# A decoder layer with 32 experts: w_down loaded once per expert, padding rows left out, the combine read with plain loads

## The reference

```python
h = rms_norm(x, g_pre_ffn[l]) * (1.0 + sc2) + sh2
y = hier_moe(h, ...)                    # below
x = x + gt2 * rms_norm(y, g_post_ffn[l])

# hier_moe: 4 groups of 8 experts, EXPERT_BLOCK = 128
group_p = softmax(ht @ w_rg + b_rg)              # top 1 group
e_prob, e_local = top_k(softmax(e_logit of that group), 2)
weights = g_prob * e_prob / sum(e_prob)
order = argsort(expert_ids)                      # 4096 assignments
padded = (counts + 127) // 128 * 128             # each expert: whole blocks of 128 rows
hb = silu(xb @ w_gate[e]) * (xb @ w_up[e])       # w_gate, w_up: 1024 x 256
y_block = hb @ w_down[e]                         # w_down: 256 x 1024
out = zeros.at[sorted_tok].add(y_sorted * weights)
```

## Time and profile before

| | us |
|---|---|
| median of 3 runs | 1963.77 |
| the profiled execution | 1967.04 |
| its span, first to last instruction | 1965.6 |
| PE busy | 1591.6 (81%) |
| DVE busy | 1313.0 (67%) |
| ACT busy | 844.5 (43%) |
| POOL busy | 260.1 (13%) |

### The profile page before, as it was taken

The page is one execution under the profiler, slowest core; times in us unless marked ns, Lnnn a source line. Parts: engine busy times, 40 slices in busy tenths (PEclk is TensorE's granted clock), DMA queues, the critical chain, the costliest instruction groups (busy, mean ns, idle before and its releaser), DMA issues. The chain is left out here.

```text
span 1965.6 us, 23849 instructions
## 1 busy us (share of the span) xinstructions
PE 1591.6 (81%) x7295; PEld 1179.9 (60%) x7296; DVE 1313.0 (67%) x1996; ACT 844.5 (43%) x1458; POOL 260.1 (13%) x382
## 2 busy tenths in 40 slices
PE   2698665799997999988999989377898888989800
PEld 2578544689565887657894644355676666766500
DVE  5399866599754699554996422675676666767556
ACT  1422330432545233534325323045666676767544
POOL 1000000000110000200001102121222222222164
PEclk7799856799987999978999889579999899999955
DMA  9254222231442332422311426459888878788677
GB/s 342 58 183 150 65 77 116 65 98 53 130 128 66 86 108 86 126 89 65 105 46 57 115 64 171 150 186 361 322 291 316 314 280 290 283 284 328 224 245 268
DMA packets 207655, 333.69 MB, mean 170 GB/s; under 512 B 7454, under 2 KB 155035, under 8 KB 207578
## 3 DMA queue, kind: packets, MB, share of 16 engines
q0 software_dynamic: 48704, 181.57, 27.3%
q1 hardware_dynamic: 158754, 151.09, 23.3%
q10 hardware_dynamic: 120, 0.04, 0.0%
HBM read 265.56 MB, written 67.11 MB: 169 GB/s over the span
## 5 line engine op out<-in xcount | busy, mean ns | idle before, releaser
L1634 DVE TENSOR_TENSOR w_rest<-wgu,w_high 128x1024 fp32r<-128x1024 f32 x192 | 232.1, 1221 | 168.2 <-ACT w_high L1560 167.3
L886 DVE SCALAR_TENSOR_TENSOR cv<-u,taps,cv 128x512 f32<-128x512 f32 x480 | 321.8, 747 | 0.6 <-DVE yT L842 0.3
L1560 ACT ACTIVATE w_high<-wgu 128x1024 fp32r x192 | 199.4, 1053 | 218.9 <-SPq L1424 156.2
L415 PE MATMUL bank<-hT_high,tiles_operand 128*128 128x512 f32 x512 | 204.5, 400 | 35.8 <-DVE hT_operand L860 21.1
L416 PE MATMUL bank<-hT_operand,tiles_operand 128*128 128x512 f32 x512 | 203.2, 397 | 0.0
L417 PE MATMUL bank<-hT_high,win_operand 128*128 128x512 f32 x512 | 202.4, 395 | 0.0
L438 PE MATMUL bank<-wo,yT 128*128 128x512 f32 x432 | 194.3, 606 | 0.0
L1520 PE MATMUL py<-wd,hTe 128*128 128x512 f32 x384 | 172.6, 592 | 0.6 <-DVE hTe L1657 0.6
L1509 PE MATMUL pgu<-w_high,x_high 128*128 128x512 f32 x384 | 161.1, 420 | 0.0
L1510 PE MATMUL pgu<-w_rest,x_high 128*128 128x512 f32 x384 | 155.5, 405 | 0.0
L1511 PE MATMUL pgu<-w_high,x_rest 128*128 128x512 f32 x384 | 153.6, 400 | 0.0
(11 more groups left out here) (326 smaller groups left out, 2785.6 us busy)
## 6 DMA issues: line engine op xcount, KB each, us to landing
wd<-w_down_in POOLq DMA_DIRECT2D x48, 1024.0 KB, 7.2
win<-w_in_in SPq DMA_DIRECT2D x64, 512.0 KB, 5.2
wgu<-w_gate_in SPq DMA_DIRECT2D x32, 1024.0 KB, 11.4
wgu<-w_up_in SPq DMA_DIRECT2D x32, 1024.0 KB, 13.6
y_dram<-yb POOLq DMA_DIRECT2D x48, 512.0 KB, 7.7
wo<-w_ada_in POOLq DMA_DIRECT2D x8, 2048.0 KB, 9.4
win<-w_in_in SPq DMA_DIRECT2D x16, 1024.0 KB, 5.3
y_dram<-zeros POOLq DMA_DIRECT2D x32, 512.0 KB, 7.7
```

What stands on the lines that cost most here:

```text
L415: nc.tensor.matmul(out[:], high[:, k, cols], hT_high[:, k, :], start=(k == 0), stop=False)
L886: ins = V.scalar_tensor_tensor(out=cv[:, j], in0=u[:, j, w:w + T], scalar=tap, in1=cv[:, j], op0=ALU.mult, op1=ALU.add)
L1560: A(w_high[:, QK * q:QK * q + QK, :], c.wgu[:, bass.ds(slot, 1), QK * q:QK * q + QK, :].rearrange("p a k n -> p (a k) n"), ACT.Copy).then_ ...
L1634: V.tensor_tensor(w_rest[:, part, :], c.wgu[:, bass.ds(slot, 1), part, :].rearrange("p a k n -> p (a k) n"), w_high[:, part, :].bitcast(F3 ...
```

## The change

- Experts are numbered by rank: the rank-th expert that has rows (the first three are always listed). Three tables, made in the routing, give the rank and slot of a block, the expert of a rank and the last block of a rank. The number of blocks is rounded up to even by giving the last expert one more.
- w_down has three slots, like gate/up, and is loaded by SP once per expert. SP's order per rank is in `serve`. PE reads the rank's table before every `down` (`rank_of`).
- Padding rows get a token number out of bounds, which the gather skips (`bounds_check`); `xg` is zeroed once. A block's result is scattered to y by assignment (k x 2048 + token) with an indirect store that skips padding. No zeros are stored any more.
- The combine reads the two halves of y with plain loads on SP, 8 buffers deep.
- In the mixer the bias is added by DVE when the logits are saved, so that the matmul of L456 goes, and `outputs` makes the full-width matmuls of all heads first, then those of the one half, then those of the other.
- The semaphores of the mixer are cleared at the routing.

```diff
@@ mixer, PE @@
                 for k in range(KD):
-                    nc.tensor.matmul(out[:, 0:NR], yt[:, i % 2, k * P:(k + 1) * P], c.wroute[:, k, :], start=(k == 0), stop=False)
-                nc.tensor.matmul(out[:, 0:NR], c.ones[0:1, :], c.brow[:], start=False, stop=True).then_inc(logit_ready, 1)
+                    last = nc.tensor.matmul(out[:, 0:NR], yt[:, i % 2, k * P:(k + 1) * P], c.wroute[:, k, :], start=(k == 0), stop=(k == KD - 1))
+                last.then_inc(logit_ready, 1)
...
+                cols_of = lambda h: slice(h * P, (h + 1) * P)
                 for h in range(NH):
-                    hc = slice(h * P, (h + 1) * P)
-                    nc.tensor.matmul(pO[:, hc], c.scoreT[:, i % 2, hc], v[:, i, hc], start=True, stop=False, skip_group_check=True)
-                    for s in range(2):
-                        at = i * P + s * CH
-                        last = nc.tensor.matmul(pO[s * CH:(s + 1) * CH, hc], qd[:, h, at:at + CH],
-                                                c.state[:, (2 * i + s) % 4, hc], start=False, stop=(s == 1), skip_group_check=True)
+                    nc.tensor.matmul(pO[:, cols_of(h)], c.scoreT[:, i % 2, cols_of(h)], v[:, i, cols_of(h)],
+                                     start=(h == 0), stop=False, skip_group_check=True)
+                for s in range(2):
+                    at = i * P + s * CH
+                    for h in range(NH):
+                        last = nc.tensor.matmul(pO[s * CH:(s + 1) * CH, cols_of(h)], qd[:, h, at:at + CH],
...
@@ routing @@
             for e in range(WSLOTS):
                 load_gate_up(sp, ap, c, e, e)
+                load_down(sp, ap, c, e, e)
...
-            L(V.tensor_tensor(cmp_[:], x32[2][:].unsqueeze(1).to_broadcast([P, TAB, NE]), bc(blk[:], NE), ALU.is_le))
-            L(V.tensor_reduce(etab[:], cmp_[:], axis=AX.X, op=ALU.add))
...
+            V.tensor_copy(c.rank_expert[:], pk[:, 0:NE])
+            V.tensor_copy(c.rank_end[:], pk[:, NE:2 * NE])
+            V.tensor_copy(c.block_rank[:], pk[:, 2 * NE:2 * NE + TAB])
...
+            L(V.tensor_scalar(c.block_assign[:], pi[:, 0:TAB], float(2 * SEQ), None, ALU.add))
+            L(V.tensor_scalar(c.block_token[:], c.block_assign[:], 2 * SEQ + SEQ - 1, None, ALU.bitwise_and))
...
@@ experts, SP @@
-            def announce(s, turn):
-                sp.wait_ge(c.w_in[s], 32 * turn)
-                sp.sem_inc(gate_up_loaded, 1)
-
-            def replace(e, s):
-
-                last = sp.value_load(c.block_end[0:1, bass.ds(e, 1)], min_val=1, max_val=4 * NBLK + 1)
-                wait_apart(sp, w_rest_ready, last, sp_passed)
-                load_gate_up(sp, ap, c, e + WSLOTS, s)
+            def announce(loaded, landed, n):
+                sp.wait_ge(landed, n)
+                sp.sem_inc(loaded, 1)
+
+            def next_gate_up(r, s):
+
+                e = expert_at(r + WSLOTS)
+                wait_apart(sp, w_rest_ready, 4 * end_of(r) + 1, sp_passed)
+                load_gate_up(sp, ap, c, e, s)
+
+            def next_down(r, s):
+
+                e = expert_at(r + WSLOTS)
+                wait_apart(sp, y_ready, 2 * end_of(r) + 1, sp_passed)
+                load_down(sp, ap, c, e, s)
...
+            def serve(r, s, turn):
+                early = isinstance(r, int) and r < WSLOTS
+                announce(gate_up_loaded, c.gu_in[s], 32 * turn)
+                if isinstance(r, int) and r == WSLOTS:
+                    for n in range(2):
+                        next_down(n, n)
+                announce(down_loaded, c.wd_in[s], 16 * turn)
+                if not isinstance(r, int) or r + WSLOTS < NE:
+                    next_gate_up(r, s)
+                if not early and (not isinstance(r, int) or r - 1 + WSLOTS < NE):
+                    next_down(r - 1, (s - 1) % WSLOTS)
...
+            with sp.Fori(2, ROUNDS) as g:
+                for s in range(WSLOTS):
+                    serve(g * WSLOTS + s, s, g + 1)
+                load_x1(g)
...
@@ experts, POOL @@
-            def load_down(b, s):
-                e, _ = expert_of(pool, b)
-                pool.dma_start(c.wd[:, s], ap["w_down"][0][bass.ds(e, 1)].rearrange("a (k p) n -> p (a k) n", p=P)).then_inc(wd_in[s], 16)
-
-            def store(b, s):
+            def store(b, s, n):
+                if not (isinstance(n, int) and n == 0):
+                    wait_apart(pool, y_stored[s], 16 * n, pool_passed)
+                nc.gpsimd.tensor_copy(places[:, s:s + 1], c.block_assign[:, bass.ds(b, 1)]).then_inc(place_copied, 1)
+                pool.wait_ge(place_copied, b + 1)
                 wait_apart(pool, y_saved, 2 * b + 3, pool_passed)
-                pool.dma_start(ap["y"][bass.ds(b * P, P), :], yb[:, s]).then_inc(y_stored[s], 16)
+                pool.indirect_dma_start(ap["y"], bass.IndirectOffsetOnAxis(places[:, s:s + 1], 0), yb[:, s], None,
+                                        bounds_check=2 * SEQ - 1, oob_is_err=False).then_inc(y_stored[s], 16)
...
@@ experts, PE @@
-            def down(b, s, times):
+            def down(b):
+                r, slot = rank_of(pe, b)
                 pe.wait_ge(hT_ready, b + 1)
-                pe.wait_ge(wd_in[s], 16 * times)
+                pe.wait_ge(down_loaded, r + 1)
                 pe.wait_ge(y_saved, 2 * b + 1)
...
@@ combine @@
-        RING = 4
+        RING = 8
...
+            def load(i, s):
+                for k, (buf, done) in enumerate(((ya, ya_in), (yb, yb_in))):
+                    sp.dma_start(buf[:, s], ap["y"][k * SEQ + i * P:k * SEQ + (i + 1) * P, :]).then_inc(done[s], 16)
+
+            for s in range(RING):
+                load(s, s)
+            for i in range(NTILES):
                 wait_apart(sp, out_ready, i + 1, sp_passed)
-                sp.dma_start(out[bass.ds(i * P, P), :], c.x1_all[:, bass.ds(i, 1)].rearrange("p a n -> p (a n)")).then_inc(out_stored, 16)
+                sp.dma_start(out[i * P:(i + 1) * P, :], c.x1_all[:, i]).then_inc(out_stored, 16)
+                if i + RING < NTILES:
+                    load(i + RING, i % RING)
```

More of the change, by code:

```diff
@@ L543, in last_modulation @@
                 last.then_inc(row_done, 1)
+                pe.wait_ge(bias_ready, 1)
+                nc.tensor.matmul(bank[3][:, 0:NR], c.ones[0:1, :], c.brow[0:1, :], start=True, stop=True).then_inc(row_done, 1)
                 pe.wait_ge(mod_ready, 2)
@@ L1187, in routing_phase @@
         lane, blk = sb("lane", [P, P]), sb("blk", [P, TAB])
-        token, blkrow = sb("token", [P, NTILES]), sb("blkrow", [P, 16])
+        assign, blkrow = sb("assign", [P, NA]), sb("blkrow", [P, 16])
+        here, after = sb("here", [P, 1]), sb("after", [P, 1])
         tri, one16 = sb("tri16", [P, P], BF16), sb("one16", [P, P], BF16)
@@ L1202, in routing_phase @@
         at_row, at_blk = sb("at_row", [P, RING, P]), sb("at_blk", [P, RING, TAB])
-        etab, third = sb("etab", [P, TAB]), sb("third", [P, TAB], I32)
+        dest = sb("dest", [P, 2, NTILES], I32)
+        listed, rank, upto = sb("listed", [P, NE]), sb("rank", [P, NE]), [sb(f"upto{i}", [P, NE]) for i in range(3)]
+        col, total, third = sb("col", [P, 3]), sb("total", [P, 1], I32), sb("third", [P, 1], I32)
+        spread = sb("spread", [P, 2 * NE + TAB])
         pr = ctx.enter_context(nc.psum_tensor("prank", [P, 512], F32))
@@ L1217, in _ @@
                 load_gate_up(sp, ap, c, e, e)
+                load_down(sp, ap, c, e, e)
+            numbers = [s.num for s in c.mixer_sems]
+            assert numbers == list(range(numbers[0], numbers[-1] + 1))
+            sp.sem_clear(range(numbers[0], numbers[-1] + 1))
         @block.gpsimd
@@ L1262, in _ @@
                     last.then_inc(onehot_used, 1)
+            pe.wait_ge(spread_ready, 1)
+            nc.tensor.matmul(pk[:, 0:2 * NE + TAB], c.ones[:], spread[:], start=True, stop=True).then_inc(ranks_ready, 1)
         @block.vector
@@ L1363, in _ @@
-            L(V.tensor_scalar(x32[0][:, 0:1], x32[2][:, NE - 1:NE], -1.0, None, ALU.add))
-            L(V.tensor_copy(c.rounds[:], x32[0][:, 0:1]))
-            L(V.tensor_scalar(c.rounds[:], c.rounds[:], 1, None, ALU.arith_shift_right))
+            counted, ends = x32[1], x32[2]
+            L(V.tensor_scalar(total[:], ends[:, NE - 1:NE], 1.0, None, ALU.add))
+            L(V.tensor_scalar(total[:], total[:], 1, None, ALU.arith_shift_right))
+            L(V.scalar_tensor_tensor(out=x32[0][:, 0:1], in0=total[:], scalar=2.0, in1=ends[:, NE - 1:NE], op0=ALU.mult, op1=ALU.subtract))
@@ new lines, in _ @@
+            V.tensor_scalar(c.rounds[:], total[:], -1.0, None, ALU.add)
+            L(V.tensor_tensor(counted[:, NE - 1:NE], counted[:, NE - 1:NE], x32[0][:, 0:1], ALU.add))
+            L(V.tensor_tensor(ends[:, NE - 1:NE], ends[:, NE - 1:NE], x32[0][:, 0:1], ALU.add))
+            L(V.tensor_scalar(listed[:], counted[:], 1.0, None, ALU.min))
+            L(V.memset(listed[:, 0:WSLOTS], 1.0))
```

(23 more changed lines are left out.)

162 lines of the change are left out of this document (69 added, 93 removed).

## The result

| | before | after |
|---|---|---|
| median, us | 1963.85 (1962.04 to 1965.95, 4 runs) | 1990.86 (1990.41 to 1994.23, 4 runs) |
| profiled execution, its span | 1967.0, 1965.6 | 1990.87, 1989.3 |
| start to first `down` | 1318.9 | 1291.3 |
| first to last `down` (48 blocks) | 537.6 | 611.2 |
| last `down` to the end | 109.1 | 86.8 |

The change makes the kernel slower: ratio 1.0141, 95% interval 1.0123 to 1.0158. The three stages give -27.6 + 73.6 - 22.3 = +23.7 us, the difference of the spans. The forecast was 2039 us, with -5, +95 and -15.

The account below looks back on a forecast made before the run. The prediction saw the expert stage bound by SP held before announcements, 72 us already lost. From 1967: experts +95, mixer -5, combine -15 gave 2042, less 3.3 for the median: 2039 us; range 1995 to 2085, at 64%.

Parts of the forecast that it names:

- Direction and mechanism: Experts: SP, held by `next_down`'s wait and w_down issue, announces the next expert late; slower at 0.85, expert term +95 us.
- 14 one-block ranks, 132 us: Experts: each of 14 one-block experts stalls 9.4 us (bounds 6 and 11) on `next_down`'s wait, 132 us.
- 9 longer ranks 9 us, 4 with x1 22 us: Experts: w_down issues behind longer experts stall 1 us each at 9, 5.5 each at 4 with an x1 load.
- Mixer, -5: Mixer: bias matmul -6, reordered output matmuls +2, zero stores -1, together -5 us.
- I take +2: Mixer, `outputs`: the new order ends the halves' side-by-side running, up to +26 us; taken as +2.
- -6 (0 to -9): Mixer: removing the bias matmul saves 0.6 us slow or 0.3 fast, 16 times, -6 us in all.
- Zero stores -1, registers on PE 0: Mixer: 32 fewer zero stores, -1 us (0 to -10); experts: PE's table reads before `down`, 0, at most 38.
- Routing 0: Routing: two operations of 4.8 us go, small ones of about 4.5 us come; 0 us (-2 to +3).
- Combine -15 (-5 to -28): Combine: plain SP loads into eight buffers, 78 us against 95.6, less 2 for a late scatter; -15 us.
- Rival one: Experts: w_down issue held as long as the x1 issue in all 13 longer experts; +193 us, 2137 us, 15%.
- Rival two: Experts: PE's clock does not come back between stalls of successive one-block experts; +91 us, 2130 us, 6%.
- Rival three: Experts: SP announces before ACT's slack ends, also for one-block experts; 8 stalls stay, 1940 us, 13%.

Follow-up runs that it names:

- a_first: The changed kernel with the next gate/up announcement right behind the pair's issue, ahead of x1 load and `next_down`; 1862.13 us, ratio 0.9465 to the kernel before.
- m_outputs: The kernel before with only the new matmul order in `outputs` (all heads full width, then one half, then the other); 1946.97 us, ratio 0.9894.
- m_bias: The kernel before with only the bias matmul removed and the bias added by DVE when saving the logits; 1953.52 us, ratio 0.9937.
- a_zeros: The changed kernel with the 32 zero stores put back, into a tensor nobody reads; 1993.97 us, ratio 1.0128 to the kernel before.
- b_first: The kernel before with the next expert's announcement right behind the gate/up pair, ahead of the x1 load; 1920.14 us, ratio 0.9766.

## Why the prediction was right and where it failed

- **Direction and mechanism: right.** `next_down`'s wait and place hold SP ahead of the announcement. w_down issues 7.1 to 10.1 us behind the pair of one-block ranks (forecast 8 to 9), 3.83 us behind the start of the `down` that it waits for; only at rank 3 the path is another, the wait for a landing, which the prediction did not have. a_first, which moves the announcement ahead of the x1 load, the wait and the w_down issue, takes 128 of the 145.5 lost us away. ACT's wait for SP went to 187 us, short of "about 250".
- **14 one-block ranks, 132 us: right.** The 14 were the ones that stall, with steps of 17.9 to 21.1 us and 125.3 us above 10.03 each (9.0 a step, not 9.4). How much of it is the wait and how much its place stays open: with the wait gone and SP's row kept, 109.5 us stay lost, some 30 of them by the wait for landing that came instead.
- **9 longer ranks 9 us, 4 with x1 22 us: mis-sized.** Together 20.5. The four with x1 cost 2.0, 3.9, 2.7 and 2.0 instead of 5.5 each; no x1 issue was held longer than 1.39 us. The step read the hold off the traffic of before. With r = 2 (0.7 for 2) and the x1 loads behind one-block ranks (nothing to be seen of the 2), the term is +73.6 against +95.
- **Mixer, -5: this step failed, with the largest part of the miss.** It was -27.6 by the first `down`. "I take +2" for the reorder took the time per head as the sum of its passes, and so saw nothing that sorting could save. m_outputs shows -17.5 there. The Trainium skill (TensorEngine Tiling (Array Packing), "Key Properties") says that changing the tiling mode, not just the tile, drains the engine. The rows fit it: in before a call changes between 128 x 128 and 128 x 64 tiles eight times, in after twice, and with the halves side by side in both a call is 1.04 us shorter. By that rule each of the six changes fewer is worth 0.17 us at the fast clock, an estimate (1.04 / 6). It spoke against the +2 and was not weighed. "-6 (0 to -9)" for the bias matmul left out the clock: m_bias shows -10.1 up to the routing, 6 of it in two stretches that ran at 1.00 in place of 0.80. Up to there after has 27.4 in all.
- **Zero stores -1, registers on PE 0: right.** a_zeros; PE has no hole between `hidden` and `down` in the rows of after.
- **Routing 0: within 3 us.** 78.2 to 78.0.
- **Combine -15 (-5 to -28): right side, short by 7.** DVE's idle time for y fell by 20 us.
- **Rival one (every w_down issue held)** is out: 378 ns is the median, and none behind a pair is held longer than 1.40 us. **Rival two (the clock stays low)** is out: the stage's granted clock is 0.91 (0.93 before). The Trainium skill (TensorE: Matmul & The Clock Gate, "HAM oscillation") has a kernel that idles at every tile pay the slow restart each time; five such stalls in a row cost 18.1 to 21.1 us a step here, a single one 18.3 to 19.7, so by that rule, and by the trace, each pays once and they do not add up. **Rival three (faster)** had the mixer's and combine's gain too small: without the experts' 73.6 us the rest of the change is worth 50 us, and 1862 is what the change does once SP's row is put right.

So the sum +75 against +24: 21 us of the miss in the experts, 23 in the mixer, 7 in the combine, all to the same side.

## What to carry to other kernels

In a queue that both issues loads and tells an engine that data is there, put the announcement that is wanted next ahead of every wait and every issue that can stand; removing one wait without moving it gave 43 us, and brought a wait for a landing in its place; moving the announcement with the wait kept gave 129. A load that is issued later to spare one wait can be late for the next. A change that cuts traffic and still loses time is to be read from the releaser of the waiting engine, not from the DMA share. Sort small matmuls by tile shape, and price a removed matmul by the clock of the stretch as well as by its passes.

## What the runs showed of the hardware that I had not expected

- How long an issue on SP is held is not fixed by its place: x1's median is 6673 ns before (DMA share 0.83 in the stage), 6510 in b_first (0.91), 3286 in a_first (0.76), 428 in after (0.60), and within a_first, always behind the announcement, it goes from 779 to 5418. The two kernels with the most traffic have the longest holds; which of the queued transfers makes them is not shown. The row of a_first:

```profile
L1484 SPq DMA_DIRECT2D x_all<-x_dram x8: 779/3286/5418, 1299.5 to 1659.1; - x8
```

- Full-width and half-width matmuls in turn cost 3.12 us for 24, sorted 2.57, sorted with halves side by side 2.08.
- A PE that is busy without a hole in both kernels ran 14.1 or 17.2 us over the same work, by the clock alone (1.00, 0.80), and which of the two it gets changed with one small matmul less per call.
